# A delta rule's chunk inverses: 64x64 products replaced by packed 32x32 diagonal blocks up to the fifth level

## The reference, cut to what matters

```python
a_mat = beta[..., :, None] * jnp.einsum('nbhid,nbhjd->nbhij', k, k) * dec_strict
eye = jnp.eye(CHUNK, dtype=jnp.float32)
rhs = jnp.concatenate([(beta * gam)[..., None] * k, beta[..., None] * v], axis=-1)
sol = lax.linalg.triangular_solve(a_mat + eye, rhs, left_side=True, lower=True)
```

## Time and profile before

| | |
|---|---|
| median of 3 runs | 3120.43 us (3116.61 to 3122.56) |
| the profiled execution's own time | 3119.26 us |
| its span in the profile | 3117.5 us |
| mean granted TensorE clock | 0.995 of full speed |

### The profile page before, as it was taken

How to read it: one execution, slowest core, us unless ns; L and a number is a source line. 1 busy time by engine, 2 the same in 40 slices (tenths; PEclk the granted TensorE clock), 3 DMA queues, 4 the chain that set the end, 5 groups by cost and what they waited for, 6 DMA issues and landing times. The chain is left out here.

```text
span 3117.5 us, 42355 instructions
## 1 busy us (share of the span) xinstructions
PE 3026.5 (97%) x17006; PEld 1820.6 (58%) x17006; DVE 1735.5 (56%) x2884; ACT 821.8 (26%) x1713; POOL 828.6 (27%) x651
## 2 busy tenths in 40 slices
PE   8999999999989999999999998999999999999999
PEld 4457758886565555444466756444445666665444
DVE  3445538776487775644322565215758677765323
ACT  3226524443212222412222045111111222221001
POOL 0005401102001110032122236212607465451323
PEclk9999999999999999999999999999999999999999
DMA  7110000002279997400100130112211112117534
GB/s 305 69 66 30 2 27 2 28 2 83 104 288 359 358 354 247 175 28 26 41 29 29 42 142 8 41 41 101 95 48 68 68 54 82 75 48 291 178 128 138
DMA packets 72482, 335.17 MB, mean 108 GB/s; under 512 B 10976, under 2 KB 12512, under 8 KB 58464
## 3 DMA queue, kind: packets, MB, share of 16 engines
q1 hardware_dynamic: 67680, 315.69, 27.1%
q0 software_dynamic: 4608, 16.78, 2.1%
HBM read 284.18 MB, written 48.23 MB: 107 GB/s over the span
## 5 line engine op out<-in xcount | busy, mean ns | idle before, releaser
L3715 PE MATMUL banks<-down_ring,down_sums 128*128 128x512 f32 x440 | 189.2, 592 | 0.0
L354 PE MATMUL banks<-w_in,hT 128*128 128x512 f32 (+1 forms) x384 | 157.1, 567 | 0.4 <-PEq L174 0.4
L3415 PE MATMUL banks<-hT,ffn_raw 128*128 128x512 f32 x352 | 154.8, 593 | 2.4 <-PEq L2899 1.3
L3531 DVE SCALAR_TENSOR_TENSOR ffn_acc<-ffn_u,s_ffn_taps,ffn_acc 128x1023 f32<-128x1023 f32 x88 | 131.6, 1506 | 30.4 <-ACT ffn_acc L3468 28.8
L3715 PEld LDWEIGHTS banks<-down_ring,down_sums 128*128 128x128 f32 x440 | 83.6, 190 | 105.2 <-issue 103.8
L816 POOL TENSOR_TENSOR prob<-prob,softmax_columns 128x640 f32<-128x640 f32 (+1 forms) x64 | 75.4, 1199 | 259.6 <-DVE softmax_columns L772 259.6
L2124 PE MATMUL banks<-hT,side_ring 128*128 128x512 f32 x256 | 128.3, 621 | 1.3 <-PEq L2676 1.3
L354 PEld LDWEIGHTS banks<-w_in,hT 128*128 128x128 f32 x384 | 72.0, 190 | 77.1 <-issue 77.1
L1645 PE MATMUL banks<-expert_wd,expert_hT 128*128 128x512 f32 x256 | 112.7, 593 | 1.2 <-DVE expert_y L1744 1.2
L3415 PEld LDWEIGHTS banks<-hT,ffn_raw 128*128 128x128 f32 x352 | 66.7, 190 | 78.2 <-issue 75.1
L1584 POOL DMA_INDIRECT expert_sums<-expert_y,idxT x15 | 23.8, 1584 | 291.9 <-DVE expert_y L1744 291.9
(11 more groups left out here) (669 smaller groups left out, 6667.9 us busy)
## 6 DMA issues: line engine op xcount, KB each, us to landing
down_ring<-in_w_down SPq DMA_DIRECT2D x132, 256.0 KB, 2.9
expert_wg<-in_w_gate SPq DMA_DIRECT2D x16, 2048.0 KB, 8.2
expert_wu<-in_w_up SPq DMA_DIRECT2D x16, 2048.0 KB, 12.8
expert_wd<-in_w_down SPq DMA_DIRECT2D x16, 2048.0 KB, 12.4
ffn_raw<-in_w_ffn SPq DMA_DIRECT2D x22, 1024.0 KB, 6.3
wmod_slab<-in_w_mod SPq DMA_DIRECT2D x6, 2048.0 KB, 7.7
act_rows<-ffn_acc SPq DMA_DIRECT2D x22, 512.0 KB, 2.6
act_rows<-act_rows SPq DMA_DIRECT2D x22, 512.0 KB, 8.4
```

The source lines that it names most:

```text
L354: last = nc.tensor.matmul(c.ps[:, base + a:base + b], h[:, q, :], k.w_in[i][:, q, 0:b - a], start=q == 0, stop=q == KD - 1)
L3415: last = nc.tensor.matmul(c.bank(fi), wt[:, q, :], x[:, q, :], start=q == 0 and m != 2, stop=q == 3, skip_group_check=True)
L3531: nc.vector.scalar_tensor_tensor(acc[:, fi, g, j:SEQ], u[:, g, fi, 0:SEQ - j], k.ffn_taps[:, (f * 2 + g) * 4 + 2 - j:(f * 2 + g) * 4 + 3 - j],
L3715: return nc.tensor.matmul(c.bank(4 * (p % 2) + t), stationary_of(s)[:, P * t:P * t + P], w[s % RING][:, 0, :], start=j == 0, stop=j == N - 1)
```

## The change

Up to the fifth level all blocks that matter lie in the 32x32 diagonal blocks of the 64x64 systems. The new kernel keeps only these: `LT`, `Lm`, `X`, `U` and `T` have 128 columns instead of 256, and hold the 16 diagonal blocks of a token tile (4 heads by 4 groups `g` of 32 partitions). The products of levels 0 to 4 are 16 of 32x32 instead of 8 of 64x64. The last level works only on the block that couples the two halves of a chunk, kept apart in `far`: 8 products of 32x32 for t1 and 8 for z. The whole inverse is put together in a tensor `full`, which is set to zero once by POOL.

- PE: levels 0 to 4 run 16 products where 8 ran, of half the size each way; level 5 runs 8 of 32x32 where 8 of 64x64 ran. The number of fill products between them stays, and fin is the same but for the name of its input.
- ACT: the copies into `T` have 128 columns.
- POOL: five masks per tile instead of six, of 128 columns, and one memset of `full`.
- DVE: `LT` is written by four instructions of 32 partitions and `far` by two (`kept_blocks`), where one wrote `LT`; `X` and `U` have 128 columns; at level 4 `U` goes into `full` by four instructions of 32 partitions (`placed_blocks`), and at level 5 the far block by two (`last_blocks`).
- t1 waits for `base` or `sub` first and for `masked` second (it was the other way round), and t1 of the last level doesn't wait for `masked`.
- The constants `level` (5 by 32 columns instead of 6 by 64) and `ident_s` (32 columns, new) change, and the address `A` is fixed so that later areas stay where they were.

The core of the diff, cut:

```diff
-                    for h, r, rows in each_chunk():
-                        last = nc.tensor.matmul(own(bank(t, 0), h, r), own(Lm[:, t % 2, 0, :], h, r), k.ident_c[rows, :], start=True, stop=True)
+                    for h, g in each_block():
+                        last = nc.tensor.matmul(sub_block(bank(t, 0), h, g), sub_block(Lm[:, t % 2, 0, :], h, g), k.ident_s[rows_of(g), :],
+                                                start=True, stop=True)
...
-                        pe.wait_ge(masked, masked_upto(t, l))
                         if l == 1:
                             pe.wait_ge(base, t + 1)
                         else:
                             pe.wait_ge(sub, at_level(t, l - 1) + 1)
-                        for h, r, rows in each_chunk():
-                            last = nc.tensor.matmul(own(bank(t, 0), h, r), own(Lm[:, t % 2, l % RING, :], h, r), own(X[:, t % 2, :], h, r),
-                                                    start=True, stop=True)
+                        if l < LV - 1:
+                            pe.wait_ge(masked, masked_upto(t, l))
+                            for h, g in each_block():
+                                last = nc.tensor.matmul(sub_block(bank(t, 0), h, g), sub_block(Lm[:, t % 2, l % RING, :], h, g),
+                                                        sub_block(X[:, t % 2, :], h, g), start=True, stop=True)
+                        else:
+                            for h, g, low in each_far_block():
+                                last = nc.tensor.matmul(sub_block(bank(t, 0), h, low), sub_block(far[:, t % 2, :], h, g),
+                                                        sub_block(X[:, t % 2, :], h, g), start=True, stop=True)
...
-                            for h, r, rows in each_chunk():
-                                last = nc.tensor.matmul(own(bank(t, 2), h, r), own(U[:, t % 2, :], h, r), own(T[:, t % 2, :], h, r), start=True,
-                                                        stop=True)
+                            for h, g in each_block():
+                                nc.tensor.matmul(sub_block(bank(t, 1), h, g), sub_block(T[:, t % 2, :], h, g), sub_block(U[:, t % 2, :], h, g),
+                                                 start=True, stop=True)
+                            for h, g in each_block():
+                                last = nc.tensor.matmul(sub_block(bank(t, 2), h, g), sub_block(U[:, t % 2, :], h, g),
+                                                        sub_block(T[:, t % 2, :], h, g), start=True, stop=True)
+                        else:
+                            for h, g, low in each_far_block():
+                                last = nc.tensor.matmul(sub_block(bank(t, 1), h, g), sub_block(T[:, t % 2, :], h, low),
+                                                        full[rows_of(low), t % 2, C * h + HALF:C * h + C], start=True, stop=True)
...
-                        nc.scalar.activation(T[:, t % 2, :], bank(t, 0), ACT.Identity).then_inc(t1_out, 1)
+                        nc.scalar.activation(T[:, t % 2, :], bank(t, 0, S), ACT.Identity).then_inc(t1_out, 1)
...
+            def kept_blocks(t):
+                for g in range(GROUPS):
+                    p = rows_of(g)
+                    nc.vector.tensor_tensor(hs(LT[p, t % 2, :]), columns_of(bank(t, 1)[p, :], g % 2), columns_of(EK[p, t % 2, :], g % 2), ALU.mult)
+                for g in (0, 2):
+                    p = rows_of(g)
+                    last = nc.vector.tensor_tensor(hs(far[p, t % 2, :]), columns_of(bank(t, 1)[p, :], 1), columns_of(EK[p, t % 2, :], 1), ALU.mult)
+                last.then_inc(at, 1)
+
+            def placed_blocks(t):
+                for g in range(GROUPS):
+                    p = rows_of(g)
+                    last = nc.vector.tensor_tensor(columns_of(full[p, t % 2, :], g % 2), hs(U[p, t % 2, :]), hs(bank(t, 1, S)[p, :]), ALU.subtract)
+                last.then_inc(sub, 1)
+
+            def last_blocks(t):
+                for g in (0, 2):
+                    p = rows_of(g)
+                    last = nc.vector.tensor_scalar(columns_of(full[p, t % 2, :], 1), hs(bank(t, 1, S)[p, :]), -1.0, None, ALU.mult)
+                last.then_inc(sub, 1)
```

More of the change, by code:

```diff
@@ L39 @@
 CHUNK = 64
+HALF = CHUNK // 2
 HS, DS = 8, 64
@@ L2483, in delta_inverse @@
                                     "z", "sub", "final", "uv_out", "wt_out", "link"))
-    gtri, gK, gQ, EK, EQ, LT, Lm, U, X, T = w
+    gtri, gK, gQ, EK, EQ, LT, far, Lm, U, full, X, T = w
     LV, RING, C = 6, 4, CHUNK
-    W = GH * C
+    W, S = GH * C, GH * HALF
+    GROUPS, cleared = P // HALF, c.sem("inv_cleared")
     def bank(t, b, n=W):
@@ L2495, in own, with hs, rows_of, sub_block @@
         return x[C * r:C * r + C, C * h:C * h + C]
+    def hs(x):
+        return x.rearrange("p (h n) -> p h n", h=GH)
+    def rows_of(g):
+        return slice(HALF * g, HALF * g + HALF)
+    def sub_block(x, h, g):
+        return x[rows_of(g), HALF * h:HALF * h + HALF]
+    def columns_of(x, a):
+        return hd(x)[:, :, HALF * a:HALF * a + HALF]
     def each_chunk():
         return ((h, r, slice(C * r, C * r + C)) for h in range(GH) for r in range(2))
+    def each_block():
+        return ((h, g) for h in range(GH) for g in range(GROUPS))
+    def each_far_block():
+        return ((h, 2 * r, 2 * r + 1) for h in range(GH) for r in range(2))
     def at_level(t, l):
@@ L2526, in rows @@
                 pool.sem_inc(spread, 1)
+            nc.gpsimd.memset(full[:, :, :], 0.0).then_inc(cleared, 1)
             def mask(t, l):
@@ L2603, in _ @@
                     for h, r, rows in each_chunk():
-                        nc.tensor.matmul(bank(t, 1, BANK)[rows, P * h:P * h + P], own(U[:, t % 2, :], h, r), vb[rows, t, h, :], start=True, stop=True)
+                        nc.tensor.matmul(bank(t, 1, BANK)[rows, P * h:P * h + P], own(full[:, t % 2, :], h, r), vb[rows, t, h, :], start=True, stop=True)
                     for r in range(2):
@@ L2607, in _ @@
                             rows = slice(C * r, C * r + C)
-                            last = nc.tensor.matmul(bank(t, 2 * r)[:, C * h:C * h + C], kbg[rows, t, h, :], own(U[:, t % 2, :], h, r), start=True,
+                            last = nc.tensor.matmul(bank(t, 2 * r)[:, C * h:C * h + C], kbg[rows, t, h, :], own(full[:, t % 2, :], h, r), start=True,
                                                     stop=True)
@@ L2659, in _ @@
                         if l < LV - 1:
-                            nc.vector.tensor_tensor(X[:, t % 2, :], X[:, t % 2, :], bank(t, 2), ALU.subtract)
-                        nc.vector.tensor_tensor(U[:, t % 2, :], U[:, t % 2, :], bank(t, 1), ALU.subtract).then_inc(sub, 1)
+                            nc.vector.tensor_tensor(X[:, t % 2, :], X[:, t % 2, :], bank(t, 2, S), ALU.subtract)
+                        if l < LV - 2:
+                            nc.vector.tensor_tensor(U[:, t % 2, :], U[:, t % 2, :], bank(t, 1, S), ALU.subtract).then_inc(sub, 1)
+                        elif l == LV - 2:
+                            placed_blocks(t)
+                        else:
+                            last_blocks(t)
                 for t in pair:
@@ L3841, in second_block @@
     k.second_in, k.n_second = c.sem("second_in"), len(loads)
-    A = at[0]
-    assert A <= k.F
+    A = k.F + 5680 - 8192
+    assert at[0] <= A <= k.F
     k.x_dram = nc.dram_tensor("x_rows", (SEQ, D), F32).ap()
@@ L4005, in layout_second @@
     lv = [((r >> l) + 1 == (o >> l)) & ((r >> l) % 2 == 0) for l in range(6)]
-    x["level"] = np.ascontiguousarray(np.stack(lv, 1).astype(np.float32))
+    x["level"] = np.ascontiguousarray(np.tile(np.stack(lv[:5], 1)[:HALF, :, :HALF], (P // HALF, 1, 1)).astype(np.float32))
+    x["ident_s"] = np.tile(np.eye(HALF, dtype=np.float32), (P // HALF, 1))
 def constants(c, k, d):
```

29 lines of the change are left out of this document (15 added, 14 removed).

## The result

The changed kernel takes 3133.98 us (median of 12 runs, 3117.73 to 3148.37) against 3118.61 us for the kernel before (12 runs, 3116.61 to 3122.68): ratio 1.0049, 95% interval 1.0036 to 1.0062. The forecast was 3096 us with 3088 to 3111 around it. The sign was wrong and the time lies outside the range.

A forecast was written before the change was run, and what follows sets the result against it. PE's queue was taken to bound the stage. Per pair 5.49 (sweeps) + 0.84 (level 5) + 0.55 (shape changes) - 0.84 (waits) = 6.04 us, 24.2 us for four: 3096 us, range 3088 to 3111.

The forecast's parts named there:

- What bounds the kernel: Stage of the inverses: PE is busy 181.0 of 182.8 us, so a shorter PE queue shortens the stage.
- What a sweep costs: Levels 0 to 4: four diagonal 32x32 places run together, eight steps of 0.032 us, 0.256 us a sweep against 0.467.
- rivals 1 and 2: Sweeps: only two places run together, 0.51 us, 3123 us, chance 0.07; or one at a time, 1.02 us, 3177 us, 0.08.
- The Trainium skill's two rules: PE products: different row tiles cannot access one PSUM bank together; a matmul costs about 60 cycles however few its columns.
- rival 3: Handing out 64 instructions a sweep to PE limits: 0.012 us a pair, sweep 0.38 us, 3109 us; chance 0.13.
- Rival 4: Short products on a quarter of the array lower the granted clock; at 80 us, 16 us slower, 3136 us; chance 0.04.
- the fills stay: Argument against a falling clock in the stage: the fill products remain, half of PE's time.
- The waits: PE waiting for DVE at level 5 and before the last products: 0.48 and 0.36 us more, 0.84 us a pair.
- The wait for `placed_blocks`: Level 4 to 5: five DVE instructions a tile, 1.0 us, make PE wait 0.48 us for the second t1.
- Rival 5: DVE's small instructions cost 0.40 us, 0.32 between starts; waits grow from 0.84 to about 2.6 us a pair; 3103 us.
- The low end of my range: Whole kernel: sweep 0.22 us and no waits, 10 us more gained, 3088 us, called less likely in full.

The follow-up runs named there:

- transposed version: The change with X made by a DVE transpose of U, dropping z's second product and level 0's product, fills as in the change: 3086.9 us, ratio 0.9893 to before.
- 16-bit form: The change with the level products reading only the upper 16 bits of each number, half the instructions a product: 3104.9 us, ratio 0.9953 to before.
- runs of 1024: The kernel before with one run of 512 tiny products (1024 PE instructions, unread results) behind level 3 of each pair: 3174.9 us, ratio 1.0176.
- spread version: The change with its 20 fill products a pair spread over the levels, one left behind the last products: 3108.3 us, ratio 0.9961 to before.

## Why the prediction was wrong

**What bounds the kernel: right.** PE's queue bounds the stage, and a shorter queue would have shortened it.

**What a sweep costs: right in its mechanism, a tenth too small.** Four diagonal places in one bank do run together: 64 loads for both tiles' t1 take 0.64 us (from 1611.25) against 0.6 forecast (rivals 1 and 2 wanted 1.0 and 2.0). In z a sweep takes 0.28 us, and a level that isn't held up 4.07, not 3.8; over 16 levels that is 4 us. The Trainium skill's two rules (TensorEngine Tiling, Restrictions and Gotchas, and Instruction Overhead), which I had let stand against the change with 8 in 100, would have cost 34 to 56 us that never came: a record starts every 9 ns in a sweep (0.28 us for 32), where my estimate from the 60 cycles was 25. The four places write different partitions of the bank; what places with partitions in common do, no run shows.

**The step that failed: handing out, rival 3.** I had both ends of it in the text: 0.007 us for a pair of load and matmul in a burst and 0.029 us sustained, and then took 0.012 as if it were a price of each pair, and 3109 us. The measured limit is 3.75 / 128 = 0.029 us a pair, the far end, but as a mean over a stretch, with some 90 to 190 pairs in hand. That is why the rows of before could not show it: a 64x64 sweep needs a pair each 0.029 us, yet a level with its fills only one each 0.05. What had to be asked was not how fast a sweep can go but how many instructions a level needs in its time: 200 in 5.2 us before, 38 per us, 392 in 4.07 us after, 96 per us, against 68. By that sum a pair's levels hold 26 x 64 + 4 x 32 instructions in their sweeps and 44 in their fills, 1836, which take 27.0 us to arrive; the levels' own work is 21.3 us (four of 4.07, level 5 of 3.3, level 0 with its fill 1.7). That leaves 5.7 us a pair, 23 in all, nearly the whole gain. Measured are 21.9; that it comes so near is luck in part, since the sum leaves out the 180 to 380 instructions in hand when a run begins, worth 2.6 to 5.6 us each time at 68 per us. It could have been read ahead: the instruction queue is a row of the page, and the Trainium skill's section ISA Cache (Advanced Engine Details and Errata), which I did not weigh, names the 256 and the two lines.

**Rival 4, the clock, was real and not alone.** I gave it 4 in 100 and 80 us at half clock for it. The profiled run has 24 us in the stage and 10.2 at the scan's start; by the line through the runs the clock costs 14 us. I had put "the fills stay" against it. That the fills hold the clock is borne out (more of them between the small products, less half clock), but two a level were too few here; they were enough in the transposed version, with a third of the small products gone. Whether low clock comes from the pauses or from the short products can't be put down to one: it fell where hardly anything paused (16-bit form), and in the starved stretches of the runs of 1024 too.

**The waits: right in kind, one of them too small.** Before the last products PE's loads wait 0.55 us in each pair for `last_blocks` (2.2 us in four) instead of 0.19: the 0.36 us more that was forecast. The wait for `placed_blocks` (0.48 forecast) was 0.89 us where no pause stood before it, in the third and fourth pair; this is the fourth:

```profile
1729.22 1.17 DVE L2686 TENSOR_TENSOR inv_full<-inv_U,banks 32x128 f32<-32x128 f32 x4
...
1730.44 0.44 PE L2614 MATMUL banks<-inv_X,inv_far 32*32 32x32 f32 x16 [0.89 <-DVE inv_full L2686]
```

Its four instructions of 32 partitions start 0.28 to 0.30 us apart (four in 1.17 us) and not 0.20 as I had it; so DVE needs 1.40 us a tile instead of 1.0. In the 16-bit form, with shorter sweeps to cover it, the wait is 1.1 us in each pair (1.3 from start to start). Rival 5 was right in that much: 128-column instructions of DVE do take 0.28 to 0.29 us and not 0.40, but these small ones start no closer together than they last.

**The sum again, for the profiled stage.** Forecast 183.5 - 24.2 = 159.3 us. To it come the pauses, 26.5 less the 3.4 of waits already in the forecast: 23 (21.9 of supply, 1.3 of DVE); the longer sweeps, 4; half clock, at most half of 24: 12. That is 198 against the 197.6 measured; behind the stage come 3 us more, with the scan's start at half clock. The clock's part is a bound, not a measurement. (The low end of my range says 10 us more gained; its terms, 0.036 us on each of 30 sweeps and 0.84 us of waits a pair, give under 8, which is what 3088 stands for.)

**What stays open:** what exactly makes the granted clock fall, in the stage and in the scan behind it. One thing goes along with the latter: with three fill products behind the last products the scan's start had 0 to 3.4 us of half clock in seven kernels and 10.2 in the change; with one or none it had 13.7 to 20.5, in four. Each is one profiled execution, and no run tests it by itself. Open is also whether the 3.75 us depends on what else the DMA engines do, since the stage's DMA share is 0.1 or less in all these runs.

## What to carry to other kernels

Where a change cuts products into smaller ones that run side by side, count PE's instructions per us over the whole stretch, loads and matmuls, and twice of each at full precision: here PE could draw on 68 per us for long and on many more for a few hundred. Above that a faster product buys only a pause with "issue" as its releaser; then spread the long products between the short ones, or drop short ones. Look for what the small form makes possible elsewhere, too: here it was a transpose on DVE, worth 21 us on top of the 12 that the spread version won.

## What the hardware showed that I had not expected

- PE's instructions come in blocks of 256. Once what was there is used up, blocks start 3.5 to 4.0 us apart, mostly 3.75; the 256 themselves go through in 1.0 us. After a pause PE goes on 1.2 to 1.6 us after a 16 KB packet of the instruction queue has landed.
- DVE instructions of 32 partitions and 128 columns, four in a row, start 0.28 to 0.30 us apart; two of 128 partitions and 128 columns start 0.20 us apart.
- 32x32 products in four diagonal places that write one bank start 7 to 9 ns apart on average over a sweep, load and matmul, at 16 bits and at full precision.
- The granted clock halves in stretches of 3.4 to 20.5 us, in stages in which PE is busy for 87% of the time (the change) or 93% (the 16-bit form), and at the start of the scan, where PE is busy all the time.
